# Three output projections of a transformer block recast as seven block products per pair of tiles

## The chip, the cores and the metric

The kernel runs on one core of one Trainium2 chip. The metric is the device time of one launch in microseconds. PE is TensorE, DVE is VectorE, ACT is ScalarE, POOL is GpSimd and SP is the engine that issues most transfers.

## The reference

Everything is fp32. The first block works on 528 tokens (16 meta tokens and 512) of width 1024; only its middle bears on this change:

```
y_conv = silu(layer_norm(conv(...))) @ w_conv_out              # 528x1024 @ 1024x1024
o      = layer_norm(rwkv7_recurrence(...), per head of 64)     # GN_EPS = 64e-5
o      = (o + sum(r * k * r_k) * v) * g
y_rwkv = o @ w_rwkv_out                                        # 528x1024 @ 1024x1024
y      = gate_c * y_conv + gate_r * y_rwkv
h      = layer_norm(ALPHA * h + y @ w_o)                       # 528x1024 @ 1024x1024
h      = layer_norm(ALPHA * h + conv_gated_mlp(h))
```

A second block of attention, gated mixing and experts follows, which the change leaves as it is.

## The kernel before

**Layout.** Activations stand transposed in one SBUF array: 8 tiles (KT) of 128 features by 528 tokens (T1), each split for PSUM into two chunks of 264 (C1). Weights stream through two slots, a slab of 1024x512 at a time, each slot reloaded when the products of its slab are complete (`stream`). Each engine runs its own instruction list in program order, and the lists meet at semaphores.

**A dense stage.** `products` (L350) makes one output tile after the other: 8 matmuls (k = 0..7) for each of the two chunks, 16 in all, then `acc_full`. `take` on ACT copies the finished 128x528 tile out of PSUM and counts `acc_free`. An fp32 matmul stands in the profile as two MATMUL records.

**A stage of seven products.** `ffn_up` and `ffn_down` already work another way (`seven_products`, L459). A pair of output tiles over the two token chunks is a 2x2 block matrix product; it is made from 7 block products of 4 matmuls each (28 in place of 32) and from sums and differences of blocks: of weights on POOL (`seven_first_sums` L428, `seven_last_sum` L437, three sums before the third product and one after the second), of activations on DVE (`token_sum`), and of results. Of the results ACT copies three out of PSUM (`seven_copy`, L499), DVE adds three (`seven_c11`, `seven_c22`, `seven_c12`, L513 to L531), and ACT copies the last (`seven_last`). A pair has three PSUM banks a, b and c. PE takes the seven in the order a, b, a, c, a, c, a. Its waits inside the pair matter here:

```
pe.wait_ge(S("acc_free"), free - 1)      # before the first
pe.wait_ge(S("sv_cp"), 3*p.g + P_DONE)   # before the third: the first is copied
pe.wait_ge(S("sv_cp"), 3*p.g + Q_DONE)   # before the fifth: the third is copied
pe.wait_ge(S("acc_free"), free + 1)      # before the seventh: seven_c22 has read bank a
```

`acc_free` counts two per pair: one from `seven_c22`, one from ACT's last copy. The next pair's first product also waits for `seven_c22` (free - 1).

**The head norm beside conv_out.** After the recurrence each of the 8 tiles of its output is normed. For tile i: `gn_sum` (PE, 2 matmuls, L2615) makes the mean, `gn_center` (DVE, L3086) subtracts it, `gn_square` (ACT, L2801) squares, `gn_squares` (PE, 2 matmuls, L2623) makes the variance, DVE adds the epsilon (L3101, `gn_var`), `gn_root` (ACT, L2805) takes the root, DVE takes the reciprocal (L3103), DVE multiplies (L3105, `gn_norm`), `gn_affine` (ACT, L2810) scales and shifts, and `gn_gated` (DVE, L3090 and L3093, two operations) adds the bonus and multiplies by the gate, giving `gn_o`. The reciprocal has one buffer for all tiles. PE weaves the matmuls into conv_out: after each output tile t it issues the squares of tile t + 1 and the sum of tile t + 2 (`gn_beside`, L2626); ACT does its share after each copy. Ahead of it, `g_up` makes the gate's 8 tiles (L2565, L2566).

**After it.** `rwkv_out` waits for all eight `gn_o`. DVE multiplies conv_out's tiles by their gates (L3114), rwkv_out's by theirs and adds both (L3118, L3121, `merged`). `w_o` starts from `merged`, DVE adds its tiles to the residual (L3124, `res1`), and layer norm ln1 (`ln_pe`, from L560) waits for all of them. The gates come back from DRAM in two transfers behind conv_out's first slab (L2289).

Of the kernel before, what the change touches and what calls it, by code (L numbers as in the profile page):

```python
# [185 lines left out]
def build(nc, I, out):  # L186
# [11 lines left out]
    def sb(off, n, p0=0, p1=P):  # L198
        return A[p0:p1, off:off + n]
# [56 lines left out]
    def pc(name, i=0, p1=P):  # L256
# [16 lines left out]
    SG1, SG2, LAMC, SUBC = PAR + 904, PAR + 920, PAR + 936, PAR + 938  # L273
    OMU = PAR + 940
    h2_dram = [nc.dram_tensor("h2_x", (SEQ, D), F32, kind="Internal").ap(),
               nc.dram_tensor("h2_c", (CTX, D), F32, kind="Internal").ap()]
# [8 lines left out]
        "g_up": Dense(1, 8, 2, two, dmas=0),  # L285
        "conv_out": Dense(2, 4, KT, two), "rwkv_out": Dense(2, 4, KT, two), "w_o": Dense(2, 4, KT, two),
        "ffn_up": Seven(11, 4, KT, two, dmas=2), "ffn_down": Seven(4, 2, FT, two, cols=P),
# [155 lines left out]

    def token_sum(n, t0, x, t):

        tt = nc.vector.tensor_tensor
        if n == 1:
            ins = tt(t(1), x(0, 1), x(0, 0), ALU.subtract)
        elif n == 2:
            nc.vector.wait_ge(S("sv_t"), t0 + 1)  # L450
            ins = tt(t(2), x(1, 1), t(1), ALU.subtract)
        elif n == 3:
            ins = tt(t(3), x(1, 1), x(0, 1), ALU.subtract)
        else:
            nc.vector.wait_ge(S("sv_t"), t0 + 2)
            ins = tt(t(4), x(1, 0), t(2), ALU.subtract)
        ins.then_inc(S("sv_t"), 1)

    def seven_products(pe, p, sums, x, t, cn, t0, first=None, between=None):  # L459

        h = p.kt // 2
        a, b, c = seven_banks(p)
        free = FREE0 + p.tile
        block = seven_landed(pe, p, second=False)
        s1, s2 = sums(p)
        ready = t0 if callable(t0) else lambda i: (S("sv_t"), t0 + i)
# [29 lines left out]
        pe.wait_ge(*ready(4))
        product(a, block(1, 1), t(4), False).then_inc(S("acc_full"), 2)
# [1718 lines left out]
    def _(sp):  # L2216
# [65 lines left out]
        sp.dma_start(at(GUP[2], BW, 0, 32), I["g_up"][0][P:, BW:]).then_inc(S("g_up_in"), 16)  # L2282

        def gates_back(n):
            if n == 0:
                for q in range(4):
                    sp.wait_ge(S(f"gate_out{q}"), 16 * N_GATE // 4)
                for h in range(2):
                    sp.dma_start(at(K_ + h * KT * T1, KT * T1).rearrange("p (g t) -> p g t", t=T1),  # L2289
                                 gate_dram[h * KT:(h + 1) * KT].rearrange("g p t -> p g t")).then_inc(S("gates_in"), 16)  # L2290
        stream(sp, "conv_out", slabs(I["w_conv_out"][0], 0), pre=[(S("wk_o"), NCH)], beside=gates_back)
        stream(sp, "rwkv_out", slabs(I["w_rwkv_out"][0], 0))
        stream(sp, "w_o", slabs(I["w_o"][0], 0))
# [42 lines left out]
    def _(pe):  # L2336
# [281 lines left out]
        def gn_squares(i):  # L2618
            pe.wait_ge(S("gn_sq"), i + 1)
            if i:  # L2620
                pe.wait_ge(S("gn_var"), i)
            for c in range(2):
# [15 lines left out]
        g_up_tile(7)  # L2638
        products(pe, "conv_out", lambda k, c0, cn: at(CS + k * T1 + c0, cn), beside=gn_beside)
        products(pe, "rwkv_out", lambda k, c0, cn: at(R_ + k * TP + PADT + c0, cn), [(S("gn_o"), KT)])  # L2640
        products(pe, "w_o", lambda k, c0, cn: at(B_ + k * T1 + c0, cn), first=lambda k: (S("merged"), k + 1))
        ln_pe(pe, hk, T1, [(S("res1"), KT)])
# [14 lines left out]
    def _(act):  # L2657
# [154 lines left out]
        def gn_beside(t):  # L2812
# [15 lines left out]
        take(act, "conv_out", lambda i, acc, j: nc.scalar.activation(halves(at(i * T1 + B_, T1)), acc, ACT.Copy),
             beside=gn_beside)
        take(act, "rwkv_out", lambda i, acc, j: nc.scalar.activation(halves(at(i * T1 + A_, T1)), acc, ACT.Copy),  # L2830
             pre=[(S("gn_o"), KT)])
        take(act, "w_o", lambda i, acc, j: nc.scalar.activation(halves(at(i * T1 + A_, T1)), acc, ACT.Copy),
             pre=[(S("merged"), KT)])
        affine = lambda n: lambda k: nc.scalar.activation(  # L2834
# [41 lines left out]
    def _(pool):  # L2876
# [13 lines left out]
        for n in range(NCH):  # L2890
# [9 lines left out]
            for level in range(2, LEVELS):  # L2900
                if JOINS * n + level > 2:
                    pool.wait_ge(S("wk_y"), JOINS * n + level - 2)
                nc.gpsimd.tensor_tensor(by_head(W_AL[level % 2]), known, over_heads(sb(LVL + level * CH, CH), KT), ALU.mult)\
                    .then_inc(S("wk_al"), 1)
        up_weights()

    @block.vector
    def _(dve):
# [142 lines left out]
        for c in range(-1, NCH):  # L3051
# [36 lines left out]
        def gn_gated(i):  # L3088
# [21 lines left out]
        dve.wait_ge(S("gates_in"), 32)  # L3110
        for i in range(KT):
            dve.wait_ge(*taken("conv_out", i + 1))
            y = at(B_ + i * T1, T1)
            step(V.tensor_tensor(y, y, at(K_ + i * T1, T1), ALU.mult))  # L3114
        for i in range(KT):
            dve.wait_ge(*taken("rwkv_out", i + 1))
            z = at(A_ + i * T1, T1)
            step(V.tensor_tensor(z, z, at(K_ + (KT + i) * T1, T1), ALU.mult))  # L3118
            step.done()
            y = at(B_ + i * T1, T1)  # L3120
            V.tensor_tensor(y, y, z, ALU.add).then_inc(S("merged"), 1)  # L3121
        for i in range(KT):
            dve.wait_ge(*taken("w_o", i + 1))
            V.scalar_tensor_tensor(out=at(hk(i), T1), in0=at(hk(i), T1), scalar=ALPHA, in1=at(A_ + i * T1, T1),  # L3124
                                   op0=ALU.mult, op1=ALU.add).then_inc(S("res1"), 1)
        V.memset(A[:, UB:UB + 4 * UW].rearrange("p (i t) -> p i t", t=UW)[:, :, 0:FFN_K - 1], 0.0).then_inc(S("ffn_zero"), 1)
# [114 lines left out]
```

## Time and profile before

| | |
|---|---|
| median of 3 runs | 4411.53 us (4407.86 to 4412.85) |
| profiled execution, its own time | 4412.77 us |
| its span | 4410.9 us |
| mean granted PE clock | 0.979 of full |
| PE busy | 4124.3 us, 94% of the span |
| DVE busy / ACT busy / POOL busy | 1510.5 / 1032.0 / 566.4 us |

The span runs from the first to the last instruction of the profiled execution. A busy PE is one with a matmul somewhere in its pipeline. Times in the rows are microseconds from the start of the span unless marked ns.

### The profile page before, as it was taken

The numbers are of one execution on the slowest core, as the hardware profiler recorded it, in microseconds if no ns is written. First come the engines' busy times: TensorE is split into PE (matmuls) and PEld (weight loads), VectorE is DVE, ScalarE is ACT, GpSimd is POOL, SyncE is SP. The second block draws the span as 40 slices with busy tenths as digits, with TensorE's granted clock in tenths as the row PEclk, the third lists the DMA queues.
The fourth block names the chain that finished last, engine by engine and source line by source line (L and its number), as shares of the span: only waits on it lengthen the run. The fifth ranks groups of instructions, "written<-read, shape, count | busy, mean of one in ns | idle before, by whom it ended". The sixth has DMA issues, their size and how long they took to land. (4 is left out here: it accounts for less than half of the span.)

```text
span 4410.9 us, 64037 instructions
## 1 busy us (share of the span) xinstructions
PE 4124.3 (94%) x28220; PEld 2665.5 (60%) x28220; DVE 1510.5 (34%) x2344; ACT 1032.0 (23%) x2078; POOL 566.4 (13%) x476
## 2 busy tenths in 40 slices
PE   7999999999999889898999889999899989969888
PEld 5888789887888646555555433433355468833332
DVE  1386755353444221506533400000314164421112
ACT  2112522211111220605311311211315052121111
POOL 0000022101451000002333111000000024400000
PEclk9999999999999999999999989999999999989999
DMA  2584300212232211010111399999211111279997
GB/s 88 176 282 164 87 23 4 81 58 71 81 105 72 70 42 46 25 38 20 38 58 58 138 353 386 390 389 357 101 39 51 38 39 69 85 311 426 427 427 314
DMA packets 191432, 664.59 MB, mean 151 GB/s; under 512 B 11558, under 2 KB 75750, under 8 KB 166582
## 3 DMA queue, kind: packets, MB, share of 16 engines
q1 hardware_dynamic: 184950, 638.24, 38.2%
q0 software_dynamic: 6208, 22.27, 1.7%
q8 instruction: 224, 3.67, 0.3%
q14 instruction: 50, 0.41, 0.0%
HBM read 638.85 MB, written 20.05 MB: 149 GB/s over the span
## 5 line engine op out<-in xcount | busy, mean ns | idle before, releaser
L473 PE MATMUL psum<-arena 128*128 128x264 f32 (+2 forms) x4312 | 1083.6, 414 | 12.0 <-ACT arena L2834 6.7
L473 PEld LDWEIGHTS psum<-arena 128*128 128x128 f32 x4312 | 817.7, 190 | 274.6 <-issue 12.7
L372 PE MATMUL psum<-arena 128*128 128x264 f32 (+4 forms) x3232 | 869.1, 429 | 35.2 <-ACT arena L1308 19.1
L372 PEld LDWEIGHTS psum<-arena 128*128 128x128 f32 x3232 | 612.9, 191 | 278.2 <-issue 120.3
L1198 PE MATMUL psum<-arena 128*64 128x512 f32 x3072 | 702.0, 604 | 44.6 <-DMA arena<-in_w_e 38.0
L1198 PEld LDWEIGHTS psum<-arena 128*64 128x64 f32 x3072 | 212.9, 138 | 470.9 <-issue 430.3
L2067 DVE TENSOR_TENSOR arena<-arena,psum 128x512 f32<-128x512 f32 x32 | 22.0, 688 | 805.6 <-PE psum L1204 546.1
L876 PE MATMUL psum<-arena 128*128 128x512 f32 x544 | 235.8, 592 | 0.0
L505 ACT ACTIVATE arena<-psum 128x384 f32<-128x384 f32 (+2 forms) x246 | 103.9, 422 | 561.6 <-PE psum L473 532.6
L2455 PE MATMUL psum<-arena 64*64 64x64 f32 x7424 | 225.8, 219 | 8.2 <-issue 4.5
L2455 PEld LDWEIGHTS psum<-arena 64*64 64x64 f32 x7424 | 223.9, 135 | 11.2 <-issue 8.4
L442 POOL TENSOR_TENSOR arena<-arena 128x512 f32<-128x512 f32 (+1 forms) x78 | 114.4, 1466 | 564.1 <-PE psum L473 564.1
L1204 PE MATMUL psum<-arena 128*32 128x256 f32 x3072 | 185.7, 382 | 0.0
L876 PEld LDWEIGHTS psum<-arena 128*128 128x128 f32 x544 | 103.2, 190 | 128.5 <-issue 127.7
L1204 PEld LDWEIGHTS psum<-arena 128*32 128x32 f32 x3072 | 90.0, 109 | 127.4 <-issue 77.9
L2932 DVE SCALAR_TENSOR_TENSOR arena<-arena 128x528 f32<-128x528 f32 x240 | 164.8, 761 | 0.0
L2085 DVE SCALAR_TENSOR_TENSOR arena<-psum,arena 128x512 f32<-128x512 f32 (+1 forms) x96 | 66.9, 706 | 188.5 <-PE psum L1165 168.4
L525 DVE TENSOR_TENSOR arena<-arena,psum 128x384 f32<-128x384 f32 (+2 forms) x82 | 38.5, 469 | 267.0 <-PE psum L473 267.0
L432 POOL TENSOR_TENSOR arena<-arena 128x512 f32<-128x512 f32 (+1 forms) x78 | 95.0, 1218 | 249.6 <-DMA arena<-in_ffn_up 237.6
L2410 PE MATMUL psum<-arena 128*128 128x264 f32 x512 | 117.4, 387 | 0.0
L1582 ACT ACTIVATE arena<-psum,arena 64x512 f32<-64x512 f32 x64 | 43.7, 683 | 292.9 <-PE psum L1204 167.1
L2410 PEld LDWEIGHTS psum<-arena 128*128 128x128 f32 x512 | 96.1, 189 | 19.2 <-ACT arena L2743 2.5
(386 smaller groups left out, 3885.9 us busy)
## 6 DMA issues: line engine op xcount, KB each, us to landing
arena<-in_w_e SPq DMA_DIRECT2D x192, 2048.0 KB, 16.1
arena<-in_w_in SPq DMA_DIRECT2D x38, 2048.0 KB, 8.0
arena<-in_w_ada SPq DMA_DIRECT2D x24, 2048.0 KB, 8.7
arena<-in_ffn_up SPq DMA_DIRECT2D x22, 1024.0 KB, 7.5
arena<-in_w_branch SPq DMA_DIRECT2D x6, 2048.0 KB, 7.8
arena<-in_ffn_down SPq DMA_DIRECT2D x8, 1408.0 KB, 7.2
arena<-in_w_in SPq DMA_DIRECT2D x16, 512.0 KB, 4.5
arena<-in_w_out SPq DMA_DIRECT2D x4, 2048.0 KB, 8.1
```

The lines of the kernel that those rows point to most:

```text
L372: mm = pe.matmul(PS[0:m, 2 * region + c, 0:cn], w[0:kp, k, j * P:j * P + m], rhs(k, c0, cn), start=(k == 0), stop=(k == s.kt - 1))
L432: tt(s1, block(1, 0), block(1, 1), ALU.add).then_inc(S("sv_sum"), 1)
L442: tt(a12, a12, sums(p)[1], ALU.subtract).then_inc(S("sv_sum"), 1)
L473: mm = pe.matmul(PS[:, bank, 0:cn], w[:, k, :], tile, start=fresh and k == 0, stop=k == h - 1, skip_group_check=not fresh)
L505: nc.scalar.activation(dst, PS[:, c if made == M5 else a, 0:cn], ACT.Copy).then_inc(S("sv_cp"), 1)
L876: mm = pe.matmul(PS[:, 2 * r, :], at(tokens + t * P, P), w[:, k, :], start=(k == 0), stop=(k == KT - 1))
L1198: mm = pe.matmul(PS[c * HD:c * HD + HD, b + (m > 0), :], x(kk), w[:, k, c * BW:c * BW + BW], start=(kk == 0), stop=(kk == KT - 1))
L1204: mm = pe.matmul(PS[c * 32:c * 32 + 32, b + 2, (m > 0) * CTX:(m > 0) * CTX + CTX], xc(kk), w[:, k, c * CTX:c * CTX + CTX], start=(kk == 0) ...
L2085: inc(V.scalar_tensor_tensor(out=x, in0=PS[:, 6 + i % 2, 0:cn], scalar=mod(5, i, kind), in1=x, op0=ALU.mult, op1=ALU.add), "moe_res")
L2410: mm = pe.matmul(PS[:, 6 + c, 0:C1], at(gate_w[g % 3] + k * P, P), rhs_h(k, c * C1, C1), start=(k == 0), stop=(k == KT - 1))
L2455: mm = pe.matmul(PS[p0:p0 + HD, bank, i * CH:i * CH + CH], lhs(i, p0), rhs(i, p0), start=(j == 0), stop=(j == len(terms) - 1))
L2932: nc.vector.scalar_tensor_tensor(out=at(ck(k), T1), in0=at(j + ak(k), T1), scalar=pc("conv_w", n), in1=at(ck(k), T1), op0=ALU.mult, op1=AL ...
```

## The change

conv_out, rwkv_out and w_o become `Seven` stages: four pairs each. POOL gets the weight sums of 12 pairs. DVE makes conv_out's activation sums at once (4 operations of 4 tiles each, after the recurrence's last products), and those of rwkv_out and w_o tile by tile (`tile_sums`: one operation of 128x264 for tiles 0 to 3, three for tiles 4 to 7). The head norm's PE work is woven in at two points of each conv_out pair: after the second product (`between`) and after the fifth (`late`). The root reads PSUM itself, with the epsilon as its bias, so that L3101 is gone. DVE's additions for conv_out's pair n stand in the norm's loop, behind the tile 2n + 2. The second half of the gates goes into the place of conv_out's input, when conv_out is complete.

```
-        "conv_out": Dense(2, 4, KT, two), "rwkv_out": Dense(2, 4, KT, two), "w_o": Dense(2, 4, KT, two),
+        "conv_out": Seven(2, 4, KT, two), "rwkv_out": Seven(2, 4, KT, two), "w_o": Seven(2, 4, KT, two),
...
+    def tile_sums(k, n, x, t, done):
+        tt, h = nc.vector.tensor_tensor, KT // 2
+        tile = lambda i: t(i)[:, k % h, :]
+        if k < h:
+            tt(tile(1), x(0, 1)[:, k, :], x(0, 0)[:, k, :], ALU.subtract).then_inc(S(done), 1)
+        else:
+            b21, b22 = x(1, 0)[:, k - h, :], x(1, 1)[:, k - h, :]
+            nc.vector.wait_ge(S(done), h)
+            tt(tile(2), b22, tile(1), ALU.subtract).then_inc(S(done), 1)
+            tt(tile(3), b22, x(0, 1)[:, k - h, :], ALU.subtract).then_inc(S(done), 1)
+            nc.vector.wait_ge(S(done), h + 3 * (n - h) + 1)
+            tt(tile(4), b21, tile(2), ALU.subtract).then_inc(S(done), 1)
...
@@ seven_products
         product(a, block(1, 0), t(3), False).then_inc(S("sv_pe"), 1)
+        if late:
+            late()
...
+    def proj_adds(dve, base, n, p):
+        seven_c11(dve, p, proj_parts[0], C1, proj_half(base, n, 0, 0))
+        seven_c22(dve, p, proj_parts[2], C1, proj_half(base, n, 1, 1))
+        seven_c12(dve, p, proj_parts[1], C1, proj_half(base, n, 0, 1))
+
+    def proj_copies(act, base, n, p, beside=()):
+        for i, (made, part) in enumerate(zip((M1, M6, M5), proj_parts)):
+            seven_copy(act, p, made, part, C1)
+            if beside and i == 0:
+                beside[0](2 * n)
+        if beside:
+            beside[0](2 * n + 1)
+        a = seven_last(act, p)
+        nc.scalar.activation(proj_half(base, n, 1, 0), PS[:, a, 0:C1], ACT.Copy).then_inc(S("acc_free"), 1)
...
@@ SP
+        def gates_more(n):
+            if n == 0:
+                sp.wait_ge(S("acc_full"), FULL0 + st["conv_out"].tile1)
+                gates_half(1)
         stream(sp, "conv_out", slabs(I["w_conv_out"][0], 0), pre=[(S("wk_o"), NCH)], beside=gates_back)
-        stream(sp, "rwkv_out", slabs(I["w_rwkv_out"][0], 0))
+        stream(sp, "rwkv_out", slabs(I["w_rwkv_out"][0], 0), beside=gates_more)
...
@@ PE
-                pe.wait_ge(S("gn_var"), i)
+                pe.wait_ge(S("gn_sd"), i)
...
+        for n, p in enumerate(conv7):
+            seven_products(pe, p, proj_sums, conv_x, conv_t, C1, lambda i: (S("conv_t"), i),
+                           between=lambda: gn_beside(2 * n), late=lambda: gn_beside(2 * n + 1))
+        for n, p in enumerate(rwkv7):
+            seven_products(pe, p, proj_sums, rwkv_x, rwkv_t, C1, tile_sums_ready("rwkv_t"),
+                           first=None if n else lambda k: (S("gn_o"), k + 1))
+        for n, p in enumerate(w_o7):
+            seven_products(pe, p, proj_sums, w_o_x, w_o_t, C1, tile_sums_ready("w_o_t"),
+                           first=None if n else lambda k: (S("merged"), proj_order.index(k) + 1))
...
@@ ACT
         def gn_root(i):
-            act.wait_ge(S("gn_var"), i + 1)
-            nc.scalar.activation(at(RSTD, T1), at(RSTD, T1), ACT.Sqrt).then_inc(S("gn_sd"), 1)
+            act.wait_ge(S("gn_sum2"), i + 1)
+            if i:
+                act.wait_ge(S("gn_norm"), i)
+            nc.scalar.activation(halves(at(RSTD, T1)), PS[:, 6:8, 0:C1], ACT.Sqrt, bias=sb(EPS, 1)).then_inc(S("gn_sd"), 1)
...
@@ DVE
+        dve.wait_ge(S("wk_o"), NCH)
+        for n in range(1, 5):
+            token_sum(n, 0, conv_x, conv_t, "conv_t")
...
         for i in range(KT):
             if i + 1 < KT:
                 gn_center(i + 1)
-            dve.wait_ge(S("gn_sum2"), i + 1)
-            if i:
-                dve.wait_ge(S("gn_norm"), i)
-            V.tensor_scalar(halves(rstd), PS[:, 6:8, 0:C1], GN_EPS, None, ALU.add).then_inc(S("gn_var"), 1)
             dve.wait_ge(S("gn_sd"), i + 1)
             step(V.reciprocal(rstd, rstd))
             step.done()
             V.tensor_tensor(gn_y(i), gn_y(i), rstd, ALU.mult).then_inc(S("gn_norm"), 1)
             if i:
                 gn_gated(i - 1)
+            if i >= 2:
+                rwkv_sums(i - 2)
+            if i >= 2 and i % 2 == 0:
+                proj_adds(dve, B_, i // 2 - 1, conv7[i // 2 - 1])
         gn_gated(KT - 1)
+        rwkv_sums(KT - 2)
+        rwkv_sums(KT - 1)
+        proj_adds(dve, B_, 3, conv7[3])
...
+        dve.wait_ge(S("gates_in1"), 16)
+        for n, p in enumerate(rwkv7):
+            proj_adds(dve, A_, n, p)
+            for i in range(2):
+                proj_tile_done(p, i)
+                k = proj_tile(n, i)
+                z, y = at(A_ + k * T1, T1), at(B_ + k * T1, T1)
+                step(V.tensor_tensor(z, z, at(GATES[1] + k * T1, T1), ALU.mult))
+                step.done()
+                V.tensor_tensor(y, y, z, ALU.add).then_inc(S("merged"), 1)
+            for i in range(2):
+                dve.wait_ge(S("merged"), 2 * n + i + 1)
+                tile_sums(proj_tile(n, i), 2 * n + i, w_o_x, w_o_t, "w_o_t")
```

## Rows read from the trace of the kernel before

**Rows 1.** Windows of three stages: length; busy (x) PE, PEld, DVE, ACT, POOL; PEclk.

```profile
873.00:943.10 70.10, 68.79 (x309) 58.43 (x309) 52.60 (x46) 21.98 (x33) 0.00 (x0) 1.00 0.21 77
943.10:1000.30 57.20, 57.20 (x257) 48.88 (x258) 14.81 (x22) 4.28 (x7) 0.00 (x0) 1.00 0.21 74
1000.30:1058.70 58.40, 56.99 (x257) 48.32 (x255) 7.11 (x11) 5.50 (x9) 0.00 (x0) 1.00 0.12 44
```

**Rows 2.** PE's waits from 873 to 1062 us: total, times, longest.

```profile
PE psum L560 <- DVE arena L3124: 1.4, 1, 1.4
PE psum L372 <- DVE arena L3093: 1.3, 1, 1.3
```

**Rows 3.** Timeline of one tile of conv_out: start, us, engine, line.

```profile
881.11 1.05 PE L2615 MATMUL psum<-arena 128*128 128x264 f32 x4
...
882.00 7.28 PE L372 MATMUL psum<-arena 128*128 128x264 f32 x32
882.20 0.70 DVE L3086 TENSOR_TENSOR arena<-arena,psum 128x528 f32<-128x528 f32 x1 [1.77 <-PE psum L2615]
...
882.94 0.64 ACT L2801 ACTIVATE arena<-arena 128x528 f32<-128x528 f32 x1 [1.19 <-DVE arena L3086]
883.55 0.64 ACT L2805 ACTIVATE arena<-arena 128x528 f32<-128x528 f32 x1
884.23 3.45 DVE L3103 RECIPROCAL arena<-arena 128x528 f32<-128x528 f32 x1 [0.71 <-ACT arena L2805]
887.72 0.71 DVE L3105 TENSOR_TENSOR arena<-arena 128x528 f32<-128x528 f32 x1
888.34 0.70 DVE L3090 TENSOR_TENSOR arena<-arena 128x528 f32<-128x528 f32 x1
...
889.08 0.71 DVE L3093 TENSOR_TENSOR arena<-arena 128x528 f32<-128x528 f32 x1
```

**Rows 4.** Timeline ahead of conv_out and at its start.

```profile
863.90 0.70 DVE L3086 TENSOR_TENSOR arena<-arena,psum 128x528 f32<-128x528 f32 x1 [11.09 <-PE psum L2615]
...
875.56 0.64 ACT L2805 ACTIVATE arena<-arena 128x528 f32<-128x528 f32 x1
```

**Rows 5.** Groups by shape in ffn_up's stretch (1100 to 1380 us).

```profile
L442 POOL TENSOR_TENSOR arena<-arena 128x512 f32<-128x512 f32 x21 | 54.2, 2581 | 127.9 <-PE psum L473 127.9
L505 ACT ACTIVATE arena<-psum 128x264 f32<-128x264 f32 x65 | 25.5, 392 | 131.8 <-PE psum L473 131.8
...
L518 DVE TENSOR_TENSOR arena<-arena,psum 128x264 f32<-128x264 f32 x22 | 9.3, 424 | 0.0
...
L3160 DVE TENSOR_TENSOR arena<-arena 128x264 f32<-128x264 f32 x11 | 4.7, 427 | 0.0
```

**Rows 6.** Timeline in ffn_up: two operations of one pair, one of the next.

```profile
1202.28 0.43 DVE L3160 TENSOR_TENSOR arena<-arena 128x264 f32<-128x264 f32 x1
1202.62 0.42 DVE L518 TENSOR_TENSOR arena<-arena,psum 128x264 f32<-128x264 f32 x1
...
1215.09 0.43 DVE L518 TENSOR_TENSOR arena<-arena,psum 128x264 f32<-128x264 f32 x1
```

**Rows 7.** Timeline: PE restarting after two of its idle stretches.

```profile
583.91 3.68 PE L2463 MATMUL psum<-arena 64*64 64x128 f32 x32 [4.59 <-DVE arena L3018]
...
1082.23 16.13 PE L473 MATMUL psum<-arena 128*128 128x264 f32 x58 [6.66 <-ACT arena L2834]
```

**Rows 8.** Windows around these and one more restart: PEclk, the granted clock.

```profile
1078.00:1082.20 4.20, 0.00 (x0) 0.00 (x1) 4.17 (x4) 0.94 (x2) 0.00 (x0) 0.50 0.00 0
1082.20:1088.00 5.80, 5.77 (x13) 4.49 (x14) 5.37 (x8) 5.19 (x8) 0.00 (x0) 0.50 0.00 0
...
583.90:589.80 5.90, 5.89 (x72) 5.90 (x74) 1.75 (x3) 0.00 (x0) 0.70 (x1) 0.50 0.36 103
...
3160.70:3163.50 2.80, 2.78 (x4) 1.20 (x5) 2.80 (x5) 2.80 (x6) 0.00 (x0) 0.50 0.00 0
```

**Rows 9.** Transfers issued from 938 to 955 us: KB each, us to landing.

```profile
arena<-in_w_rwkv_out SPq DMA_DIRECT2D x1, 2048.0 KB, 8.0
```

More of the change, by code:

```diff
@@ L274, in build @@
     OMU = PAR + 940
+    EPS = PAR + 1000
     h2_dram = [nc.dram_tensor("h2_x", (SEQ, D), F32, kind="Internal").ap(),
@@ L442, in seven_last_sum, with tile_sums_ready, token_sum @@
         tt(a12, a12, sums(p)[1], ALU.subtract).then_inc(S("sv_sum"), 1)
-    def token_sum(n, t0, x, t):
+    def tile_sums(k, n, x, t, done):
[10 more added lines that the diff above has]
+            tt(tile(4), b21, tile(2), ALU.subtract).then_inc(S(done), 1)
+    def tile_sums_ready(done):
+        h = KT // 2
+        return lambda i: (S(done), (0, h, 4 * h - 2, 4 * h - 1, 4 * h)[i])
+    def token_sum(n, t0, x, t, done="sv_t"):
         tt = nc.vector.tensor_tensor
@@ L449, in token_sum @@
         elif n == 2:
-            nc.vector.wait_ge(S("sv_t"), t0 + 1)
+            nc.vector.wait_ge(S(done), t0 + 1)
             ins = tt(t(2), x(1, 1), t(1), ALU.subtract)
@@ L454, in token_sum, with seven_products @@
         else:
-            nc.vector.wait_ge(S("sv_t"), t0 + 2)
+            nc.vector.wait_ge(S(done), t0 + 2)
             ins = tt(t(4), x(1, 0), t(2), ALU.subtract)
-        ins.then_inc(S("sv_t"), 1)
-    def seven_products(pe, p, sums, x, t, cn, t0, first=None, between=None):
+        ins.then_inc(S(done), 1)
+    def seven_products(pe, p, sums, x, t, cn, t0, first=None, between=None, late=None):
         h = p.kt // 2
@@ L2207, in build @@
     down_out = lambda n, i: DOWN_O + (2 * (n % 2) + i) * T1
+    conv7, rwkv7, w_o7 = (st[n].pairs for n in ("conv_out", "rwkv_out", "w_o"))
+    PROJ_S = K_ + KT * T1
+    PROJ_T = PROJ_S + 4 * KT // 2 * P
+    PROJ_C, PROJ_T4 = PROJ_T + 2 * KT // 2 * C1, TMP + 2064
+    assert PROJ_C + 3 * C1 <= A_ and PROJ_T4 + KT // 2 * C1 <= GUP[0]
+    GATES = [K_, CS]
+    kt4 = lambda off: at(off, KT // 2 * C1).rearrange("p (k t) -> p k t", t=C1)
+    kt_half = lambda base, pitch: lambda j, c: at(base + j * KT // 2 * pitch, KT // 2 * pitch)\
+        .rearrange("p (k t) -> p k t", t=pitch)[:, :, c * C1:c * C1 + C1]
+    conv_x, rwkv_x, w_o_x = kt_half(CS, T1), kt_half(R_ + PADT, TP), kt_half(B_, T1)
+    conv_t = lambda i: (kt4(PROJ_T), kt4(PROJ_T + KT // 2 * C1), conv_x(0, 1), kt4(PROJ_T4))[i - 1]
+    w_o_t = lambda i: (kt4(PROJ_T), kt4(PROJ_T + KT // 2 * C1), w_o_x(0, 1), kt4(PROJ_T4))[i - 1]
+    rwkv_t = lambda i: (kt4(B_ + KT * T1), kt4(B_ + KT * T1 + KT // 2 * C1), rwkv_x(0, 1), kt4(BNS + T1))[i - 1]
+    proj_sums = lambda p: [at(PROJ_S + (2 * (p.g % 2) + i) * 4 * P, 4 * P).rearrange("p (k n) -> p k n", n=P) for i in range(2)]
+    proj_parts = [at(PROJ_C + i * C1, C1) for i in range(3)]
+    proj_tile = lambda n, i: n // 2 * 4 + n % 2 + 2 * i
+    proj_order = [proj_tile(n, i) for n in range(4) for i in range(2)]
+    proj_half = lambda base, n, i, c: at(base + proj_tile(n, i) * T1 + c * C1, C1)
+    def proj_adds(dve, base, n, p):
[11 more added lines that the diff above has]
+        nc.scalar.activation(proj_half(base, n, 1, 0), PS[:, a, 0:C1], ACT.Copy).then_inc(S("acc_free"), 1)
     def in_chunk(off, c):
@@ L2282, in _, with gates_half @@
         sp.dma_start(at(GUP[2], BW, 0, 32), I["g_up"][0][P:, BW:]).then_inc(S("g_up_in"), 16)
+        def gates_half(h):
+            sp.dma_start(at(GATES[h], KT * T1).rearrange("p (g t) -> p g t", t=T1),
+                         gate_dram[h * KT:(h + 1) * KT].rearrange("g p t -> p g t")).then_inc(S(f"gates_in{h}"), 16)
         def gates_back(n):
@@ L2287, in gates_back @@
                     sp.wait_ge(S(f"gate_out{q}"), 16 * N_GATE // 4)
-                for h in range(2):
-                    sp.dma_start(at(K_ + h * KT * T1, KT * T1).rearrange("p (g t) -> p g t", t=T1),
-                                 gate_dram[h * KT:(h + 1) * KT].rearrange("g p t -> p g t")).then_inc(S("gates_in"), 16)
+                gates_half(0)
+        def gates_more(n):
+            if n == 0:
+                sp.wait_ge(S("acc_full"), FULL0 + st["conv_out"].tile1)
+                gates_half(1)
         stream(sp, "conv_out", slabs(I["w_conv_out"][0], 0), pre=[(S("wk_o"), NCH)], beside=gates_back)
-        stream(sp, "rwkv_out", slabs(I["w_rwkv_out"][0], 0))
+        stream(sp, "rwkv_out", slabs(I["w_rwkv_out"][0], 0), beside=gates_more)
         stream(sp, "w_o", slabs(I["w_o"][0], 0))
@@ L2638, in _ @@
         g_up_tile(7)
-        products(pe, "conv_out", lambda k, c0, cn: at(CS + k * T1 + c0, cn), beside=gn_beside)
-        products(pe, "rwkv_out", lambda k, c0, cn: at(R_ + k * TP + PADT + c0, cn), [(S("gn_o"), KT)])
-        products(pe, "w_o", lambda k, c0, cn: at(B_ + k * T1 + c0, cn), first=lambda k: (S("merged"), k + 1))
+        for n, p in enumerate(conv7):
[7 more added lines that the diff above has]
+                           first=None if n else lambda k: (S("merged"), proj_order.index(k) + 1))
         ln_pe(pe, hk, T1, [(S("res1"), KT)])
@@ L2818, in gn_beside @@
                 gn_root(t + 1)
-            if t == KT - 2:
+            if t == KT - 1:
                 gn_affine(KT - 1)
@@ L2827, in _ @@
         gn_root(0)
[L2828 to L2833, printed above, removed]
+        for n, p in enumerate(conv7):
+            proj_copies(act, B_, n, p, beside=[gn_beside])
+        for n, p in enumerate(rwkv7):
+            proj_copies(act, A_, n, p)
+        for n, p in enumerate(w_o7):
+            proj_copies(act, A_, n, p)
         affine = lambda n: lambda k: nc.scalar.activation(
@@ L2904, in _ @@
                     .then_inc(S("wk_al"), 1)
+        for p in (*conv7, *rwkv7, *w_o7):
+            seven_first_sums(pool, nc.gpsimd.tensor_tensor, p, proj_sums)
+            seven_last_sum(pool, nc.gpsimd.tensor_tensor, p, proj_sums)
         up_weights()
@@ L2914, in _ @@
         nc.vector.tensor_scalar(at(OMU, N_MIX), at(col["mu"], N_MIX), -1.0, 1.0, ALU.mult, ALU.add).then_inc(S("omu"), 1)
+        step(nc.vector.memset(sb(EPS, 1), GN_EPS))
+        step.done()
         ln_dve(dve, step, hk, hk, T1, LN_EPS)
@@ L3093, in gn_gated, with rwkv_sums @@
             V.tensor_tensor(gn_y(i), gn_y(i), at(A_ + i * T1, T1), ALU.mult).then_inc(S("gn_o"), 1)
+        def rwkv_sums(i):
+            dve.wait_ge(S("gn_o"), i + 1)
+            tile_sums(i, i, rwkv_x, rwkv_t, "rwkv_t")
         gn_center(0)
@@ L3107, in _ @@
                 gn_gated(i - 1)
+            if i >= 2:
+                rwkv_sums(i - 2)
+            if i >= 2 and i % 2 == 0:
+                proj_adds(dve, B_, i // 2 - 1, conv7[i // 2 - 1])
         gn_gated(KT - 1)
[L3110 to L3125, printed above, removed]
+        rwkv_sums(KT - 2)
+        rwkv_sums(KT - 1)
+        proj_adds(dve, B_, 3, conv7[3])
+        def proj_tile_done(p, i):
+            if i == 0:
+                dve.wait_ge(S("sv_c"), 2 * p.g + 2)
+            else:
+                dve.wait_ge(S("acc_free"), FREE0 + p.tile + 2)
@@ new lines, in _ @@
+        dve.wait_ge(S("gates_in0"), 16)
+        for n, p in enumerate(conv7):
+            for i in range(2):
+                proj_tile_done(p, i)
+                k = proj_tile(n, i)
+                y = at(B_ + k * T1, T1)
+                step(V.tensor_tensor(y, y, at(GATES[0] + k * T1, T1), ALU.mult))
+        dve.wait_ge(S("gates_in1"), 16)
+        for n, p in enumerate(rwkv7):
+            proj_adds(dve, A_, n, p)
+            for i in range(2):
+                proj_tile_done(p, i)
+                k = proj_tile(n, i)
+                z, y = at(A_ + k * T1, T1), at(B_ + k * T1, T1)
+                step(V.tensor_tensor(z, z, at(GATES[1] + k * T1, T1), ALU.mult))
+                step.done()
+                V.tensor_tensor(y, y, z, ALU.add).then_inc(S("merged"), 1)
+            for i in range(2):
+                dve.wait_ge(S("merged"), 2 * n + i + 1)
+                tile_sums(proj_tile(n, i), 2 * n + i, w_o_x, w_o_t, "w_o_t")
@@ L3126, in _ @@
+        for n, p in enumerate(w_o7):
+            proj_adds(dve, A_, n, p)
+            for i in range(2):
+                proj_tile_done(p, i)
+                k = proj_tile(n, i)
+                V.scalar_tensor_tensor(out=at(hk(k), T1), in0=at(hk(k), T1), scalar=ALPHA, in1=at(A_ + k * T1, T1),
+                                       op0=ALU.mult, op1=ALU.add).then_inc(S("res1"), 1)
         V.memset(A[:, UB:UB + 4 * UW].rearrange("p (i t) -> p i t", t=UW)[:, :, 0:FFN_K - 1], 0.0).then_inc(S("ffn_zero"), 1)
```

## The prediction

> **What bounds the kernel now.** The page comes first: PE is busy 94% of the span, the next engine 34%. Matmul time is what this kernel pays for, if the matmuls removed stand where PE sets the pace. So I read the windows of the three stages, which take 185.7 us together: PE is busy all of it but 2.7 us [rows 1]. PE's waits in that stretch are two, 1.3 us for the last `gn_o` and 1.4 us for the last `res1` [rows 2]. So before the change PE sets the end of all three, and DVE, busy 52.6 of conv_out's 70.1 us [rows 1], only has to keep up. It does so with little to spare, and that is what the timeline of one tile is for: it gives every link of the head norm, in order, with the delay between engines [rows 3]. The reader should see there a loop over DVE, ACT and back, of which one DVE instruction, the reciprocal, takes 3.45 us.
>
> **Grid.** Two matmuls start 0.89 us before the next group (881.11 to 882.00) [rows 3], so s = 0.445 us for one. A pair of 28 then takes 12.46 us, and ffn_up's pairs, which have this form already, repeat after 12.47 us (1202.62 to 1215.09) [rows 6]. There the copies, sums and additions cost PE nothing.
>
> **What goes.** Each stage drops from 128 to 112 matmuls: 48 x 0.445 = 21.4 us of PE. In rwkv_out and w_o I take the whole of it: 2 x 49.84 = 99.7 us. DVE has per pair three additions and two to six sums of 0.42 to 0.43 [rows 5] and four operations of 0.71, at most 6.7 us of 12.46. POOL's four sums take at most 2.58 each [rows 5], 10.3 of 12.46. rwkv_out's first additions wait for the gates' second half, which is issued when conv_out ends; a slab of about its size lands 8.0 us after its issue [rows 9], and bank a is wanted 24s = 10.7 us in, so that this hides, by about 1 us. Behind SP's wait for it only rwkv_out's second slab is queued, needed 25 us later. For w_o's third product the last activation sum has to be there: last copy 0.6 us after rwkv_out, gate and addition 1.45, sums of two tiles about 1.5, together 3.55, against 8s = 3.56. No stall. The tail after w_o's last matmul: 0.2 to ACT, copy 0.39 [rows 5], residual 0.71, latencies 0.1, in all 1.4. The two stages and tail: 101.1 us, against 57.2 + 58.4 = 115.6 [rows 1]. That is -14.5.
>
> **L3101** leaves DVE, 0.70 a tile. Before, it stood between centring and root without being the last to come in steady state; its worth is inside the chain below. The epsilon's memset lies at the start, ahead of a wait for PE.
>
> **conv_out's activation sums** need the recurrence's last products, and then 4 DVE operations of 1056 columns, nearest 0.43 x 4 = 1.7 each, 6.8 us at most. DVE idles 11.1 us before its first centring [rows 4]. They hide.
>
> **The wait that is added.** A pair's seventh product needs `seven_c22` of the same pair. DVE issues it behind the norm of tile 2n + 2, and the variance of that tile is only made in `late`, after the fifth product. Between `late`'s squares and the seventh product PE has only one `gn_sum` and four matmuls, 2.7 us. DVE has far more. From the start of one centring: 2.03 to the reciprocal (square and root on ACT, 882.20 to 884.23), 3.49 to the norm, 0.62 to the first gated operation, 0.74 to the second, 0.62 to the next: 7.50 us a tile [rows 3]. Behind it stand the sum for rwkv_out (0.35, as two such follow each other at 1202.28 and 1202.62 [rows 6]; three for tiles 4 to 7, about 1.1) and the additions (0.35, then c22 0.43 and 0.05 to PE). Queued behind PE's wait is everything of the next pair, the `gn_sum` included that DVE's next centring waits for. The loop closes.
>
> Its period, from one release X of the seventh product: 4 + 8 + 4 matmuls, 16s = 7.12; 0.20 to the centring; two tiles, 15.0; two sums, 0.70; c11 and c22 0.83. In all **23.85 us**, of which PE works 36s = 16.0 and idles 7.8. Before, two tiles took 2 x 20s = 17.8.
>
> Step by step from 873.0: the first root stands at 875.56 behind a table load [rows 4] and L3101 had not delayed it, so the first reciprocal starts at 876.24, norm 879.7, centring of tile 2 880.35; two tiles with one sum and the first additions end at X1 = 896.6. X2 = 920.5. X3 has tile 4's three sums, +0.75: 945.1. The last pair has one tile to norm, two to gate and nine sums: 14s + 0.2 = 6.43, root 0.68, reciprocal 3.49, norm 0.62, two gatings 2.7, sums 3.3, additions 0.83: X4 = 963.1. Seventh product 1.8: conv_out ends at 964.9 against 943.1. That is **+21.8**. With -14.5 it makes +7.3.
>
> **The clock.** PE stands idle four times, three times about 8 us and once 4.7 (18.1 less 30s). Where it idled 6.66 us [rows 7] the granted clock fell from 2.4 to 1.2 GHz while it waited, and stayed there for 5.8 us of work; after 4.59 us of idle [rows 7] it stood at the lower level for 5.9 us [rows 8]. Half of that time is lost, 2.9 us, and all of it lies in the loop, since PE's first 7.1 us after X are on it. 4 x 2.9 = 11.6 us. The low end is the restart at 3160.7, 2.8 us at the lower level [rows 8], 4 x 1.4 = 5.6; below that, nothing, if the clock holds. I take 2.9: two of the three restarts give it, and their idle stretches bracket these.
>
> **Sum.** 21.8 - 14.5 + 11.6 = **+18.9 us**. On the profiled execution's 4412.77 it gives 4431.7; on the median of 4411.53, which lies 1.2 lower, **4430.4 us**.
>
> **POOL beside DVE.** POOL's last weight sum takes 2.58 us on average in ffn_up, next to DVE's taps [rows 5]. In conv_out it is released by the second product, when DVE still idles, and the first sums of the next pair then fall on the reciprocal, so I take nothing. The other end: one chain operation a pair is held up by one such sum, 3 x 2.58 = 7.7 us. The Trainium skill ("SBUF — State Buffer", Who interferes with whom) has a rule against the change here: DVE's two-input operations and GpSimd take turns at a shared port, and the second blocks for the whole of the first; by it the sum would be this upper one if the turns fell badly, and the long POOL time in ffn_up agrees with a lock that POOL loses.
>
> **Rivals.**
> 1. *The loop, but the clock stays up.* For it: short waits elsewhere leave PEclk at 1.00. Against: both restarts after 4.6 and 6.7 us. 4411.5 + 7.3 = 4418.8, within the 8.8 us that are 0.2% of the time, which is about what a measurement tells from no change. Chance 0.1.
> 2. *The loop does not bind* (the other side). Place: PE's wait before the seventh product. It decides where c22 comes within 2.7 us of `late`'s squares; any DVE order that puts it before the norm of tile 2n + 2 does that. conv_out would go at PE's pace and all three stages save their matmuls: -21.4, 4390.1. Against it: the lists run in order, and the shortest road from the squares to c22 is root, reciprocal, norm, two gatings, over 6 us. Break-even is a period of 21.2 us ((185.7 - 101.1)/4) against my 23.85 without clock. Chance 0.06, misreadings of the order included.
> 3. *POOL holds up the chain.* +7.7: 4438.1. Chance 0.1.
> 4. *More clock than counted*: the lower level lasts over the whole working stretch of a pair, or the gates land late. Up to 3 us more in each of three pairs, 4440. Chance 0.08.
>
> The forecast has 0.66, its own range 4424 (low restarts) to 4433.
>
> **Range and chances.** The forecast and rivals 1 and 3 lie within 4418 to 4439 and hold 0.86 together; that is the range. Slower by over 0.2% (above 4420.4): 0.66 + 0.1 + 0.08 = 0.84. Within 0.2%: 0.1. Faster: 0.06.
>
> **What would show it.** Right: conv_out's pairs repeat every 26 to 27 us; PE's waits show about 28 us in four pieces, each before a seventh product and released by DVE's c22; PEclk 0.5 for 3 to 6 us after each; rwkv_out begins near 975; rwkv_out and w_o pairs repeat every 12.46 without waits; ln1 begins near 1077.6 instead of 1058.7. Wrong: no wait before the seventh product (rival 2), PEclk 1.00 across conv_out (rival 1), chain operations of DVE longer than before [rows 3] (rival 3), a wait in rwkv_out's first pair. The rest of the kernel should keep its lengths; if it does not, the sum is wrong from outside.

## The result, and the profile after

| | before | after |
|---|---|---|
| median (runs of this comparison) | 4412.19 us (6) | 4429.4 us (6) |
| lowest to highest | 4407.86 to 4413.95 | 4426.61 to 4435.48 |
| profiled execution | 4412.77 us | 4435.48 us |
| mean granted PE clock | 0.979 | 0.974 |

The ratio is 1.004 with a 95% interval of 1.003 to 1.0051: slower, by 17.2 us in the medians. The forecast was 4430.4 us.

**The three stages.** Windows of the changed kernel, conv_out, rwkv_out and w_o; they answer to [rows 1]. Columns: the stretch, its length, busy time (count) of PE, PEld, DVE, ACT and POOL, the granted clock, DMA share and GB/s.

```profile
877.40:979.70 102.30, 72.25 (x277) 58.73 (x277) 61.58 (x72) 22.70 (x40) 20.43 (x16) 0.82 0.12 41
979.70:1030.40 50.70, 50.70 (x225) 43.15 (x224) 19.68 (x39) 6.26 (x16) 20.05 (x16) 0.98 0.36 126
1030.40:1081.80 51.40, 50.18 (x226) 42.32 (x224) 14.60 (x30) 6.65 (x17) 16.31 (x13) 1.00 0.15 50
```

The borders are where the last product of a stage ends; they are worked out from its release, 976.09 for conv_out, and from ACT's copy of it, at 980.01 and 1030.63. conv_out went from 70.1 us, of which PE sat idle for 1.3, to 102.3, of which it sat idle for 30.0, at a mean clock of 0.82. The other two went from 57.2 and 58.4 to 50.7 and 51.4. In all 204.4 us against 185.7.

**Who PE waited for**, from 873 to 1085 us; it answers to [rows 2]. Columns: total us, times, longest.

```profile
PE psum L493 <- DVE arena L547: 28.4, 4, 8.3
PE psum L493 <- issue: 1.6, 1, 1.6
PE psum L582 <- DVE arena L3227: 1.2, 1, 1.2
```

L493 is the matmul of the seven products and L547 the addition in `seven_c22`: four waits, one a pair. The forecast had 28 us in four pieces. The 1.6 us is the one wait before a fifth product, in the first pair.

**The loop, one turn of it.** Timeline of the changed kernel, the second conv_out pair, from one release of the seventh product to the next; it answers to [rows 3]. Columns: start, duration, engine, line; in brackets the idle time before and its releaser.

```profile
901.46 0.42 DVE L547 TENSOR_TENSOR arena<-arena,psum 128x264 f32<-128x264 f32 x1
...
901.94 7.76 PE L493 MATMUL psum<-arena 128*128 128x264 f32 x24 [8.18 <-DVE arena L547]
...
911.51 0.70 DVE L3165 TENSOR_TENSOR arena<-arena,psum 128x528 f32<-128x528 f32 x1 [9.29 <-PE psum L2678]
912.25 0.64 ACT L2870 ACTIVATE arena<-arena 128x528 f32<-128x528 f32 x1 [3.19 <-DVE arena L3165]
...
912.80 0.68 ACT L2876 ACTIVATE arena<-psum,arena 128x528 f32<-128x528 f32 x1
...
913.52 3.45 DVE L3182 RECIPROCAL arena<-arena 128x528 f32<-128x528 f32 x1 [1.30 <-ACT arena L2876]
...
918.43 1.94 PE L493 MATMUL psum<-arena 128*128 128x264 f32 x8
...
921.33 3.45 DVE L3182 RECIPROCAL arena<-arena 128x528 f32<-128x528 f32 x1 [1.30 <-ACT arena L2876]
924.82 0.71 DVE L3184 TENSOR_TENSOR arena<-arena 128x528 f32<-128x528 f32 x1
...
927.49 0.42 DVE L547 TENSOR_TENSOR arena<-arena,psum 128x264 f32<-128x264 f32 x1
...
927.97 2.57 PE L493 MATMUL psum<-arena 128*128 128x264 f32 x5 [7.59 <-DVE arena L547]
```

PE's sixth product starts at 918.43 and is done at 920.4; the seventh waits until DVE has gone through the whole norm of the next tile and comes to L547. DVE in its turn sat idle 9.3 us before the centring at 911.51, for the sum that PE had queued behind its own wait. The releases lie at 901.94, 927.97, 955.32 and 976.09.

**The clock.** Windows right behind these four releases:

```profile
901.90:906.10 4.20, 4.16 (x10) 3.24 (x11) 0.32 (x1) 0.24 (x1) 0.00 (x0) 0.50 0.02 4
928.00:933.40 5.40, 5.40 (x12) 4.17 (x13) 0.25 (x1) 0.39 (x1) 0.00 (x0) 0.50 0.10 13
955.30:960.70 5.40, 5.38 (x12) 4.21 (x13) 0.30 (x1) 0.39 (x1) 0.00 (x0) 0.50 0.00 0
976.10:981.20 5.10, 5.10 (x12) 3.97 (x13) 5.10 (x9) 0.39 (x1) 0.00 (x0) 0.50 0.09 5
```

Each restart ran at 1.2 GHz, and the windows end a little before the clock rose. Slices of 0.2 us hold the rise:

```profile
906.20:906.40 0.20, 0.20 (x2) 0.18 (x1) 0.00 (x0) 0.05 (x1) 0.00 (x0) 0.68 0.00 0
933.60:933.80 0.20, 0.20 (x3) 0.17 (x2) 0.00 (x0) 0.00 (x0) 0.00 (x0) 0.91 1.01 154
960.80:961.00 0.20, 0.20 (x2) 0.20 (x1) 0.00 (x0) 0.00 (x0) 0.00 (x0) 0.65 0.00 0
981.40:981.60 0.20, 0.20 (x2) 0.15 (x2) 0.00 (x0) 0.00 (x0) 0.00 (x0) 0.94 0.34 53
```

From release to rise the lower level lasted 4.4, 5.7, 5.6 and 5.3 us, 21.0 us together, so that half of it, 10.5 us, was lost.

### The profile page after: what moved, and what is told of

Same layout as the page of the kernel before. It is cut to its first block and busy times, and to the rows that moved or that the text cites. A ratio compares the mean times of both kernels' runs of the same rounds, so it can differ in the third digit from the quotient of the medians.

```text
span 4433.6 us, 64095 instructions
## 1 busy us (share of the span) xinstructions
PE 4117.8 (93%) x28124; PEld 2655.6 (60%) x28124; DVE 1535.0 (35%) x2409; ACT 1036.4 (23%) x2102; POOL 626.3 (14%) x524
## 5 line engine op out<-in xcount | busy, mean ns | idle before, releaser
L493 PE MATMUL psum<-arena 128*128 128x264 f32 (+2 forms) x4984 | 1246.2, 413 | 42.1 <-DVE arena L547 29.0
L493 PEld LDWEIGHTS psum<-arena 128*128 128x128 f32 x4984 | 951.9, 192 | 331.8 <-DVE arena L547 31.5
L373 PE MATMUL psum<-arena 128*128 128x265 f32 (+5 forms) x2464 | 696.2, 443 | 33.8 <-ACT arena L1330 19.2
L373 PEld LDWEIGHTS psum<-arena 128*128 128x128 f32 (+1 forms) x2464 | 466.8, 191 | 251.1 <-issue 122.5
L527 ACT ACTIVATE arena<-psum 128x264 f32<-128x264 f32 (+2 forms) x282 | 117.9, 418 | 621.4 <-PE psum L493 592.6
L443 POOL TENSOR_TENSOR arena<-arena 128x512 f32<-128x512 f32 (+1 forms) x90 | 129.3, 1437 | 705.4 <-PE psum L493 705.4
L1226 PE MATMUL psum<-arena 128*32 128x256 f32 x3072 | 185.7, 382 | 0.0
L898 PEld LDWEIGHTS psum<-arena 128*128 128x128 f32 x544 | 103.2, 190 | 128.5 <-issue 127.7
L547 DVE TENSOR_TENSOR arena<-arena,psum 128x264 f32<-128x264 f32 (+2 forms) x94 | 43.6, 464 | 303.5 <-PE psum L493 303.5
L433 POOL TENSOR_TENSOR arena<-arena 128x512 f32<-128x512 f32 (+1 forms) x90 | 110.4, 1227 | 65.7 <-DMA arena<-in_w_conv_out 33.4
L2473 PEld LDWEIGHTS psum<-arena 128*128 128x128 f32 x512 | 96.1, 189 | 19.2 <-ACT arena L2812 2.5
```

The costliest lines, as they stand in the source:

```text
L373: mm = pe.matmul(PS[0:m, 2 * region + c, 0:cn], w[0:kp, k, j * P:j * P + m], rhs(k, c0, cn), start=(k == 0), stop=(k == s.kt - 1))
L433: tt(s1, block(1, 0), block(1, 1), ALU.add).then_inc(S("sv_sum"), 1)
L443: tt(a12, a12, sums(p)[1], ALU.subtract).then_inc(S("sv_sum"), 1)
L527: nc.scalar.activation(dst, PS[:, c if made == M5 else a, 0:cn], ACT.Copy).then_inc(S("sv_cp"), 1)
L898: mm = pe.matmul(PS[:, 2 * r, :], at(tokens + t * P, P), w[:, k, :], start=(k == 0), stop=(k == KT - 1))
L1226: mm = pe.matmul(PS[c * 32:c * 32 + 32, b + 2, (m > 0) * CTX:(m > 0) * CTX + CTX], xc(kk), w[:, k, c * CTX:c * CTX + CTX], start=(kk == 0) ...
```

## The experiments

All times below are medians; each kernel was compared with the kernel before on its chip, whose median there was 4413.3 to 4413.9 us. "Stage" is the time from conv_out's first matmul to ln1's first, from the profiled execution.

| kernel | median | ratio to before (95%) | stage |
|---|---|---|---|
| before | 4412.19 | | 185.7 |
| after | 4429.4 | 1.004 (1.003 to 1.0051) | 204.4 |
| e1_adds_early | 4408.06 | 0.9991 (0.9982 to 1.0) | 181.3 |
| e2_filler | 4421.18 | 1.002 (1.0011 to 1.0029) | 194.1 |
| e3_conv_dense | 4396.54 | 0.9961 (0.9948 to 0.9975) | 171.3 |
| e4_root_only | 4414.0 | 1.0 (0.9991 to 1.0009) | 185.4 |
| e5_pool_placed | 4401.15 | 0.9971 (0.9961 to 0.998) | 172.6 |
| e6_tail | 4389.13 | 0.9946 (0.9932 to 0.9959) | 167.7 |

### e2: keep PE busy while it waits

```
+        if filler:
+            for _ in range(filler):
+                pe.matmul(PS[:, 3 - a, 0:cn], mean_h, x(0, 0)[:, 0, :], start=True, stop=True)
         pe.wait_ge(S("acc_free"), free + 1)
```

`filler` is 16 in the first three pairs and 9 in the last.

> The changed kernel, with 16 matmuls (9 in the last pair) of no use put ahead of each wait of the seventh product in conv_out; they write a PSUM bank that nobody reads, and fit into the idle stretches (7.1 and 4.0 us against 7.6 to 8.3 and 4.4). Clock theory: PE no longer idles long enough for the granted clock to fall, PEclk is 1.00 through the stage, a period is 23.9 to 24.5 us instead of 26.0 to 27.4, and the time falls by 9 to 12 us to about 4419 us. Rival (the clock costs little, since PE waits anyway, and the 2.5 to 3.5 us over 23.85 are something else): PEclk 1.00 and the same 4429 us as the changed kernel.

The window of the stage shows the clock at full throughout:

```profile
869.20:962.00 92.80, 88.12 (x391) 73.77 (x391) 59.72 (x69) 22.69 (x40) 20.43 (x16) 1.00 0.13 46
```

The additions of `seven_c22` (L550 there) start at 893.32, 917.20, 941.76 and 959.78, so the loop turns in 23.88, 24.56 and 18.02 us; by the rows of before it was worked out at 23.85, 24.6 and 18.1. The stage is 10.3 us shorter than in the changed kernel, where the clock windows above give 10.5. The median is 8.2 us lower, a little less than the 9 to 12 expected. The clock's share is settled by the stage: adding 57 matmuls of no use makes the changed kernel faster.

### e1: the same work on DVE, another order

```
-            if i >= 2 and i % 2 == 0:
-                proj_adds(dve, B_, i // 2 - 1, conv7[i // 2 - 1])
+            if i % 2:
+                proj_adds(dve, B_, i // 2, conv7[i // 2])
...
-        proj_adds(dve, B_, 3, conv7[3])
```

> Only DVE's order is changed: the additions of conv_out's pair n stand behind tile 2n+1 of the head norm instead of tile 2n+2. Loop theory: the seventh product then needs nothing of the norm of tile 2n+2, PE's waits of 7.6 to 8.3 us vanish (at most 1 to 2 us a pair stay), a pair of conv_out takes 17 to 18 us, DVE (15.0 of norm, 1.1 of additions, 0.7 to 2.2 of sums a pair) sets it about as much as PE (16.0), PEclk stays near 1.00 in the stage, and the whole comes to 4390 to 4400 us, below the kernel before. Rival theory (seven products are slow beside the norm whatever the order: copies on ACT, POOL at the shared memory port, PSUM banks): pairs stay above 22 us and the time above 4415 us.

The long waits of three pairs are gone: before their seventh products PE waits 0.4, 0.7 and 0.7 us instead of about 8. Taking nothing away but the order gains 21.3 us in the median and 23.1 in the stage. That is the loop shown by its removal. The last pair was not helped: its wait grew from 4.4 to 6.6 us, and the clock fell there. The numbers expected were missed too: the pair takes 19.7 us (892.29, 912.03, 931.78 for L547), not 17 to 18, and the time is 4408, not 4390 to 4400. Three DVE rows of its timeline, next to POOL's, say why:

```profile
899.08 1.77 DVE L3169 TENSOR_TENSOR arena<-arena 128x528 f32<-128x528 f32 x1
...
900.89 1.66 DVE L3172 TENSOR_TENSOR arena<-arena 128x528 f32<-128x528 f32 x1
902.47 1.49 DVE L451 TENSOR_TENSOR arena<-arena 128x264 f32<-128x264 f32 x1
```

```profile
898.55 1.74 POOL L443 TENSOR_TENSOR arena<-arena 128x512 f32<-128x512 f32 x1 [12.96 <-PE psum L493]
900.25 1.73 POOL L433 TENSOR_TENSOR arena<-arena 128x512 f32<-128x512 f32 x1
902.06 1.62 POOL L435 TENSOR_TENSOR arena<-arena 128x512 f32<-128x512 f32 x1
903.63 1.46 POOL L436 TENSOR_TENSOR arena<-arena 128x512 f32<-128x512 f32 x1
```

The three DVE operations took 0.70, 0.71 and 0.43 in the changed kernel's loop, the POOL ones 1.27. They belong to the first tile that DVE norms after `seven_c22`; the second tile's, where POOL is quiet, keep their 0.70, 0.71 and 0.42. Where both engines stream two SBUF operands, both get longer, by 3.1 us a pair on DVE. That POOL is the cause is argued here and tested in e5.

### e5: POOL's sums beside the reciprocal

e1, and in conv_out POOL waits for a root before the last sum of a pair and before the second sum of the next, so that each two run while DVE has its one-input reciprocal:

```
+            seven_first_sums(pool, ..., p, proj_sums, mid=(S("gn_sd"), 2 * n + 1) if 0 < n < 4 else None)
+            if n < 4:
+                pool.wait_ge(S("gn_sd"), 2 * n + 2)
             seven_last_sum(pool, nc.gpsimd.tensor_tensor, p, proj_sums)
```

> As e1_adds_early, and POOL's weight sums in conv_out wait for a root of the norm, so that they run beside the reciprocals: the last sum of a pair and the first of the next beside tile 2n+1's, two more beside the next tile's. Theory (e1's missing gain is the memory port that POOL and DVE's two-input operations share: three norm operations a pair took 1.5 to 1.8 us instead of 0.4 to 0.7): L3169, L3172 and L451 come back to 0.71, 0.71 and 0.43 us, the pair from 19.7 to 16.8 to 17.5 us, PE's wait of 2.5 us before the fifth product goes, and the time falls 8 to 13 us below e1, to 4395 to 4400 us. Rival (the longer operations in e1 come from PE's and ACT's traffic, not POOL's): they stay long, and the time stays near 4408 us.

```profile
908.06 3.45 DVE L3186 RECIPROCAL arena<-arena 128x528 f32<-128x528 f32 x1 [1.30 <-ACT arena L2878]
908.17 1.27 POOL L437 TENSOR_TENSOR arena<-arena 128x512 f32<-128x512 f32 x1 [6.40 <-ACT arena L2878]
909.39 1.27 POOL L438 TENSOR_TENSOR arena<-arena 128x512 f32<-128x512 f32 x1
...
912.17 0.70 DVE L3173 TENSOR_TENSOR arena<-arena 128x528 f32<-128x528 f32 x1
912.19 1.05 PE L2680 MATMUL psum<-arena 128*128 128x264 f32 x4
912.29 0.83 ACT L2883 ACTIVATE arena<-arena 128x528 f32<-128x528 f32 x1 [2.17 <-DVE arena L3188]
...
912.90 0.71 DVE L3176 TENSOR_TENSOR arena<-arena 128x528 f32<-128x528 f32 x1
...
913.53 0.43 DVE L453 TENSOR_TENSOR arena<-arena 128x264 f32<-128x264 f32 x1
```

The same three operations of the first tile behind `seven_c22` are back at 0.70, 0.71 and 0.43 us. PE's and ACT's operations stand beside them as in e1, where `gn_sum` (L2678) started at 899.10 and ACT's L2881 at 899.20; only POOL's are gone from there, so it was POOL. The pair takes 16.6 us (905.38 to 922.03 for L549), PE waits 0.4 us before a seventh product, and the 2.5 us wait before the fifth is gone with it. The stage fell by 8.7 us, the median by 6.9, to 4401.15: the effect is there, a little smaller than the 8 to 13 us that were expected of the time. What was left is the last pair, where PE still waits 4.6 us and falls to the lower clock.

### e6: the end of the norm

e5, with the last pair's additions directly behind tile 7's norm, tile 5's sums ahead of it, and POOL's last sum for conv_out, with all that follows it in POOL's list, behind those:

```
+            if i == KT - 1:
+                proj_adds(dve, B_, 3, conv7[3])
             if i:
                 gn_gated(i - 1)
...
+            if n == 3:
+                pool.wait_ge(S("rwkv_t"), 10)
```

> As e5_pool_placed, with the end of the norm put in another order: the last pair's additions stand directly behind the norm of tile 7 (before two gatings and three sums), tile 5's sums ahead of tile 7's norm, and POOL's sums that ran into DVE's sums at 930 us (two of 1.50 us instead of 0.43) wait for them. Theory: PE's wait before the last pair's seventh product falls from 4.6 us to about 1 to 2 us, the clock does not fall there (2.4 to 3 us), DVE gains the 2 us of the collision, and the whole is 3 to 6 us below e5, near 4396 us. Rival (rwkv_out's first pair then waits for the norm's last tiles instead, which DVE finishes no earlier): the wait moves behind conv_out's end and less than 2 us is gained.

```profile
940.20 10.95 PE L495 MATMUL psum<-arena 128*128 128x264 f32 x48 [1.41 <-DVE arena L549]
```

The last wait is 1.4 us and PEclk stays at full until ln1's own gap. The stage is 167.7 us, 4.8 less than e5's, within the 3 to 6 expected. The median fell by 12 us, more than the stage explains: its five runs (4387.1 to 4394.8) and e5's ten (4393.9 to 4403.9) overlap, and the two profiled executions took 4394.8 and 4393.9. e6's three fastest executions have a mean granted clock of 0.980 to 0.982 and the other two 0.979, so part of the rest can be clock outside the stage; that was not shown. It beats the kernel before by 0.54%, with an interval of 0.41 to 0.68%, and is the fastest kernel of the study.

### e3: conv_out dense again

`conv_out` back to `Dense` with the norm woven in behind each tile as before, everything else of the change kept, DVE's sums for rwkv_out included.

> conv_out goes back to 16 dense matmuls a tile with the norm woven in behind each tile, rwkv_out and w_o keep their seven products. Theory: conv_out takes its 70 us again, the other two keep 12.46 us a pair, so the time is that of the kernel before less 14.5 us, 4397 us (4394 to 4400); DVE has the sums for rwkv_out besides, which may add up to 2 us ahead of rwkv_out. Rival (the loss is not in conv_out alone, or the two later stages do not gain): above 4404 us.

4396.54 us, where 4397 was expected, and a stage of 171.3 (185.7 less 14.4). The two later stages earn the whole of their removed matmuls. One small new wait shows how POOL fares beside a stream of DVE operations:

```profile
947.15 6.33 POOL L443 TENSOR_TENSOR arena<-arena 128x512 f32<-128x512 f32 x1 [25.29 <-PE psum L493]
...
953.53 1.82 PE L493 MATMUL psum<-arena 128*128 128x264 f32 x7 [1.09 <-POOL arena L443]
```

A sum of 1.27 us took 6.33 beside L3198, eight multiplications in a row, and PE waited 1.1 us for it.

### e4: the root alone

The kernel before with the root taken from PSUM and L3101 gone.

> The kernel before with nothing but the root taken from PSUM with the epsilon as bias, DVE's addition of it gone. Theory: before the change PE paces conv_out, so no change, within 2 us of 4412 us; only the last tile's chain behind the last product is shorter by 0.7 to 1 us. Rival (the chain of the norm already counted there): 5 us or more faster.

4414.0 us, ratio 1.0 (0.9991 to 1.0009), stage 185.4: no effect. The operation removed is slack, as PE paces conv_out in the dense form; PE's wait before rwkv_out went from 1.3 to 0.9 us, 0.4 less, where 0.7 to 1 less was expected. The root itself takes 0.69 us from PSUM against 0.64.

## Why the prediction was right, point by point

- **The later stages, -14.5 us**: -14.4 in e3. In the changed kernel they take 102.1 us, 0.9 of it the tail of the last restart, against 101.1 in the sum. Pairs repeat at 12.46 us without waits. The gates' second half landed in time: the first addition behind it waited for the transfer and still started at 987.97, and `seven_c22` at 989.69 waited for PE.
- **The loop**: shown by e1, its length by e2 to 0.1 us a turn. The step held as it was put: the seventh product waits for an addition that DVE's list has behind a norm which depends on `late`.
- **The start of the loop**, X1, was 24.5 us behind conv_out's start where 23.6 was worked out. The row `884.19 1.62 DVE L3184` of the changed kernel is the cause seen, 0.9 us over its usual 0.71: POOL's L435 (883.99, 1.26 us) and L436 (885.21, 1.74 us) ran beside it.
- **The clock, +11.6 us**: 10.5 by the windows, 10.3 in e2's stage. Three of the restarts were at the lower level for 5.3 to 5.7 us and one for 4.4, where 5.8 to 5.9 had been taken.
- **Together**: the stage was forecast at 185.7 + 18.9 = 204.6 us and took 204.4. Misses of +0.9 (the loop's start) and -1.1 (the clock) cancel, so that the agreement to 0.2 us is luck.
- **Outside the stage**: the prediction took it that the rest keeps its lengths. In the profiled executions conv_out starts at 877.41 after against 873.00 before, with only a memset added ahead of it (and conv_out's own sums, which PE did not wait for). PE's restart at 58.65 is already 1.3 us later, at 59.99, and about 2 us are clock: windows of 1 us give 7.9 us lost to the lower level ahead of conv_out, against 5.8 before. PE's code at these places is the same, and so is its wait of 2.33 us just ahead of the first rows. The first two windows below are of before, the last two of after (columns as above):

```profile
178.00:182.00 4.00, 4.00 (x18) 3.42 (x19) 4.00 (x8) 0.00 (x0) 0.00 (x0) 1.00 1.03 381
593.00:601.00 8.00, 7.21 (x239) 7.08 (x235) 3.96 (x6) 1.52 (x3) 3.24 (x3) 1.00 0.02 5
...
178.40:182.40 4.00, 4.00 (x11) 3.16 (x12) 4.00 (x8) 0.00 (x0) 0.00 (x0) 0.61 1.04 387
595.00:603.00 8.00, 7.22 (x153) 7.08 (x150) 3.27 (x5) 0.60 (x1) 2.83 (x3) 0.57 0.01 3
```

  In the experiments' profiles conv_out starts anywhere from 869.27 (e2, where that restart comes at 54.47) to 876.10 (e6, at 59.97). So its start moves from one execution to another, in part with that restart and in part with where the clock falls. The remaining 1 us, and whether the change has a part in any of it, stay open. The profiled execution of after is the slowest of its six, 6 us above their median: stage and start together are 23.1 us where the profiled executions differ by 22.7, and the medians differ by 17.2, less than the stage alone. That the median forecast came within 1.0 us is in part luck.
- **Rivals**: the clock holding up (4418.8) came true only where filler held it up, e2's 4421.2. The loop not binding: excluded by the four waits. More clock than counted, or late gates: neither came, as the restarts were at the lower level for 5.7 us at most. POOL on the chain: once, 0.9 us, in the changed kernel, because its sums fell on DVE's idle time and the reciprocals as argued; but the mechanism is real, and it set e1. I had not carried it into e1's expectation, although the new order moved DVE's norm under POOL's sums.

The Trainium skill ("SBUF — State Buffer", Who interferes with whom) says that a DVE instruction with two SBUF inputs and a GpSimd instruction that reads SBUF contend for a shared port, the second being blocked for the whole of the first. The rows agree in kind: in e1 0.70 us become 1.77 beside POOL operations that take 1.73 in place of 1.27, and in e5 the one-input reciprocal keeps its 3.45 us beside POOL.

## What to carry to other kernels

Fewer matmuls only pay where PE sets the pace after the change; before adding a wait to a PE list, follow what the releasing engine has queued ahead of the release, and whether any of it depends on matmuls behind the wait. Here conv_out lost 32.2 us by it and the later stages gained 13.5; leaving conv_out dense (e3) already gave -0.4%. One moved line turned +0.4% into no loss; moving POOL's sums under one-input instructions and reordering the tail then made it -0.5%. A wait of PE costs more than its length where the granted clock falls in it, so price the restart from a row of the same trace.

## What the runs showed of the hardware

DVE and POOL lengthen each other when both stream two SBUF operands: DVE's 128x528 operation from 0.70 to 1.77 us, POOL's 128x512 one from 1.27 to 1.74, and to 6.33 beside eight DVE operations in a row. Matmuls of no use during a wait kept the clock up and made a kernel 8.2 us faster. After idle stretches of 4.4 to 8.3 us the lower clock lasted 4.4 to 5.7 us of work. Behind one and the same wait of 2.33 us the clock fell in one profiled execution (after) and held in another (before).
